# A third of layer 1's later weight pieces are split on GpSimd instead of VectorE

## The reference

```
h    = modulate(rmsnorm(x)); proj = h @ w_in        # 1024 x 3856, in three groups of columns
y    = concat(ssd(proj), attention(proj), hyena(proj))
x    = x + g1 * (y @ w_out)
x    = x + g2 * swiglu(modulate(rmsnorm(x)))        # w_gu, w_down
```

## Time and profile before

| | |
|---|---|
| median of 3 runs | 1210.33 us (1209.53 to 1211.54) |
| the profiled execution's own time | 1211.26 us |
| span of that execution | 1209.2 us |
| PE busy | 1175.9 us, 97% |
| DVE busy | 826.8 us, 68% |
| ACT busy | 527.9 us, 44% |
| POOL busy | 16.3 us, 1% |
| `w_lo` on DVE (L1861) | 220 operations, 264.2 us |

### The profile page before, as it was taken

One profiled execution on the slowest core, in us unless ns is written; L12 is line 12 of the kernel. 1 busy time (PEld: TensorE's weight loads), 2 busy tenths in 40 slices (PEclk: granted clock), 3 DMA queues, 4 the chain that ended last, 5 costly groups with the idle time before them and its releaser, 6 DMA issues. The chain is left out here.

```text
span 1209.2 us, 16485 instructions
## 1 busy us (share of the span) xinstructions
PE 1175.9 (97%) x6628; PEld 952.8 (79%) x6628; DVE 826.8 (68%) x1297; ACT 527.9 (44%) x911; POOL 16.3 (1%) x35
## 2 busy tenths in 40 slices
PE   6999999999999999999999999999989999999998
PEld 4768777787667778888887778779888788889887
DVE  5746467869766838777656666575699876776674
ACT  4534544642544532231122323264785555443454
POOL 0000000000100000000000000000000010000000
PEclk9999999999999999999999999999999999999999
DMA  9843244421012255565565454323434224655653
GB/s 337 271 136 128 89 138 132 147 70 53 18 36 70 70 173 168 184 206 191 174 220 186 163 180 160 112 71 94 136 105 123 71 71 139 191 183 184 191 175 123
DMA packets 132419, 171.35 MB, mean 142 GB/s; under 512 B 9300, under 2 KB 112374, under 8 KB 132344
## 3 DMA queue, kind: packets, MB, share of 16 engines
q1 hardware_dynamic: 131860, 170.12, 43.9%
q10 hardware_dynamic: 484, 0.18, 0.1%
HBM read 169.24 MB, written 1.05 MB: 141 GB/s over the span
## 5 line engine op out<-in xcount | busy, mean ns | idle before, releaser
L1861 DVE TENSOR_TENSOR w_lo<-w_raw,w_hi 128x1024 fp32r<-128x1024 f32 (+2 forms) x220 | 264.2, 1206 | 148.6 <-ACT w_hi L1480 146.5
L1480 ACT ACTIVATE w_hi<-w_raw 128x1024 fp32r<-128x1024 f32 (+2 forms) x220 | 228.5, 1042 | 292.5 <-DMA w_raw<-in_w_gu_dram 140.6
L736 PE MATMUL ps<-h_hi,w_hi 128*128 128x512 f32 (+1 forms) x576 | 218.4, 379 | 1.5 <-ACT gate L1788 0.8
L738 PE MATMUL ps<-h_hi,w_lo 128*128 128x512 f32 (+1 forms) x576 | 212.7, 369 | 0.0
L737 PE MATMUL ps<-h_lo,w_hi 128*128 128x512 f32 (+1 forms) x576 | 212.4, 369 | 0.0
L736 PE MATMUL ps<-f_hi,w_hi 128*128 128x512 f32 (+1 forms) x472 | 167.7, 355 | 2.1 <-DVE xT L2290 1.6
L738 PE MATMUL ps<-f_hi,w_lo 128*128 128x512 f32 (+1 forms) x472 | 162.5, 344 | 0.0
L736 PEld LDWEIGHTS ps<-h_hi,w_hi 128*128 128x128 f32 x576 | 108.5, 188 | 28.3 <-issue 9.6
L738 PEld LDWEIGHTS ps<-h_hi,w_lo 128*128 128x128 f32 x576 | 108.4, 188 | 18.8
L737 PEld LDWEIGHTS ps<-h_lo,w_hi 128*128 128x128 f32 x576 | 108.6, 189 | 17.4
L747 PE MATMUL ps<-h_hi,w_hi 128*128 128x512 f32 x320 | 113.3, 399 | 0.6 <-DVE w_lo L1861 0.6
(11 more groups left out here) (346 smaller groups left out, 1871.6 us busy)
## 6 DMA issues: line engine op xcount, KB each, us to landing
w_raw<-in_w_gu_dram SPq DMA_DIRECT2D x88, 512.0 KB, 3.6
w_raw<-in_w_in_dram SPq DMA_DIRECT2D x60, 512.0 KB, 3.7
w_raw<-in_w_down_dram SPq DMA_DIRECT2D x32, 512.0 KB, 3.5
m_even<-in_w_mod_dram SPq DMA_DIRECT2D x14, 1024.0 KB, 5.8
m_odd<-in_w_mod_dram SPq DMA_DIRECT2D x14, 1024.0 KB, 5.8
m_raw<-in_w_mod_dram SPq DMA_DIRECT2D x24, 512.0 KB, 5.5
m_first<-in_w_mod_dram SPq DMA_DIRECT2D x16, 512.0 KB, 10.4
w_raw<-in_w_out_dram SPq DMA_DIRECT2D x16, 512.0 KB, 3.4
```

What stands on the lines that cost most here:

```text
L736: mm(o, w_hi[:, i % RING, w], hi[:, 0:n], start=first and k == 0, stop=False)
L738: last = mm(o, w_lo[:, i % RING, w], hi[:, 0:n], start=False, stop=final and k == nk - 1)
L1480: A(w_hi[:, i % RING, w], w_raw[:, i % RING, w], ACT.Copy).then_inc(w_hi_done, 1)
L1861: TT(w_lo[:, i % RING, w], w_raw[:, i % RING, w], w_hi[:, i % RING, w].bitcast(F32), ALU.subtract).then_inc(w_lo_done, 1)
```

## The change

Five pieces, 125, 128, 131, 134 and 137 (the ones that DVE splits in slots 13, 16, 19, 22 and 25 of layer 1), are now split by GpSimd, with the same subtraction on the same tiles. GpSimd waits for `w_hi_done` and signals a new semaphore `w_lo_pool`. DVE skips them. Since `w_lo_done` now counts only DVE's pieces, PE's waits go through `lo_ready(count)`, which waits for the right number of each; from piece 126 on, every such wait of PE is two.

```diff
+POOL_SPLITS = [PLAN[1, "in"][0] + s + 2 for s in (13, 16, 19, 22, 25)]
...
+        w_lo_pool = sem("w_lo_pool")
...
         @block.gpsimd
...
+                for i in POOL_SPLITS if l == 1 else ():
+                    pool.wait_ge(w_hi_done, i + 1)
+                    w = slice(0, piece_cols(i))
+                    nc.gpsimd.tensor_tensor(w_lo[:, i % RING, w], w_raw[:, i % RING, w], w_hi[:, i % RING, w].bitcast(F32),
+                                            ALU.subtract).then_inc(w_lo_pool, 1)
                 p.after("hy_sq", 2)
...
+            def lo_ready(count):
+                by_pool = sum(i < count for i in POOL_SPLITS)
+                pe.wait_ge(w_lo_done, count - by_pool)
+                if by_pool > 0:
+                    pe.wait_ge(w_lo_pool, by_pool)
...
-                            pe.wait_ge(w_lo_done, i + half + 1)
+                            lo_ready(i + half + 1)
...
             def split_w(i):
-                if i < PIECES:
+                if i < PIECES and i not in POOL_SPLITS:
```

More of the change, by code:

```diff
@@ L799, in first_half @@
                     part(k, w_hi, h_hi, k == 0)
-                pe.wait_ge(w_lo_done, g + 2)
+                lo_ready(g + 2)
                 for k in range(2):
@@ L828, in h_pair @@
                 for half in range(int(first), 2):
-                    pe.wait_ge(w_lo_done, g + 2 * half + 2)
+                    lo_ready(g + 2 * half + 2)
                     def of_hi(k, c):
@@ L1139, in _ @@
                             if u == 0:
-                                pe.wait_ge(w_lo_done, i + 2)
+                                lo_ready(i + 2)
                                 pair_open(q)
@@ L1166, in part_half @@
                     if j == 0:
-                        pe.wait_ge(w_lo_done, g0 + i + 1)
+                        lo_ready(g0 + i + 1)
                     if i > 0:
@@ L1318, in _ @@
                     i = g0 + PARTS + ch
-                    pe.wait_ge(w_lo_done, i + 1)
+                    lo_ready(i + 1)
                     if ch >= 2:
```

## The result

The changed kernel took 1216.55 us (median of 6 runs, 1215.77 to 1218.21), the kernel before 1211.21 us beside it (6 runs, 1209.53 to 1212.29). The ratio is 1.0045, interval 1.0035 to 1.0056: 5.3 us slower (4.2 to 6.8). The forecast was 1213.5 with a range of 1209.2 to 1215.6: the sign is right, and the time lies 0.95 us above the range. Of the 3.05 us between forecast and result, 0.88 is the base (the kernel before had a median of 1210.33 in the runs shown and 1211.21 in these) and 2.1 is the effect itself, 5.3 instead of 3.2.

A forecast was written before the change was run, and what follows sets the result against it. PE bounds most of the kernel, DVE is nearer at 880.4 to 922; 0.76 + 0.40 + 2.18 + 2.15 - 2.28 = +3.2 us on 1211.26 gives 1214.5, median 0.93 lower: 1213.5 us, range 1209.2 to 1215.6.

The forecast's parts named there:

- Duration on GpSimd: One 1024-wide split on POOL: 2.35 us, on a line through the 256-wide and 512-wide additions.
- the dear bound of 2.94: Upper bound for one POOL split, four 256-wide additions: 2.94 us; as a rival +5.5 us, 1215.9, chance 0.08.
- Exclusion: POOL and DVE operations with two SBUF inputs exclude each other for a whole instruction; no-exclusion rival 1208.0 us, chance 0.11.
- Holds of 125, 128, 131, 134: Delays from DVE held by POOL: `em` twice, +0.76 and +0.40; split of 130, 2.18; rotations and `hbuf`, 2.15 us.
- The choice that POOL gets in behind the DVE operation in flight: For pieces 131 and 134, POOL gets in at the first end of a DVE operation: +3.2 us in all, chance 0.50.
- the rival: DVE keeps the port while its operations follow each other: holds 0.53 and 0.36, in all -0.2 us, 1210.1; chance 0.27.
- the order of asking: At the port POOL and DVE are served as they came; POOL comes 0.4 us before the split of 130.
- Relief: DVE time freed per split, 1.14 us: 131 and 134 count in full, 2.28 us; 125, 128 and 137 count 0.
- the argument that PE would then wait for the rounding of piece 141: Behind the 0.33 us wait at 921.19, PE would wait for ACT's rounding instead, so 137's relief counts 0.
- The waits: PE's 93 extra waits on `w_lo_pool`, 15 in this stage and 78 behind: 0 us; rival 1.9 us, 1215.4, chance 0.04.
- Piece 137: Rounded at 910.66, POOL to 913.1 beside DVE operations with one PSUM operand; split at 913.01 hardly touched: 0.
- a late ACT: Named as a way to be wrong: a late DVE makes ACT late too; no size given.

The follow-up runs named there:

- the kernel of its own: Separate kernel with nothing of the program: GpSimd subtractions alone, then beside four kinds of VectorE chains; 1024 columns took 2.34 us alone.
- the kernel with the relief alone: Changed kernel without the GpSimd splits: nobody makes the five rests, PE multiplies `w_hi` instead; 1207.66 us, ratio 0.9977 to the kernel before.
- the filled pause: Changed kernel with 20 matmuls, output unread, in front of the `em` product of slot 20; 1215.07 us, ratio 1.0040 to the kernel before.
- the one in which GpSimd held `hyv`: Changed kernel with only pieces 132 and 134 on GpSimd, 134 only behind DVE's `hbuf`; 1209.82 us, ratio 0.9985 to the kernel before.

## Why the prediction was right in sign and too low in size

- **Duration on GpSimd.** Predicted 2.35, measured 2.34 alone and 2.38 to 2.40 in place. The line through the two shorter sizes was the right choice, and the dear bound of 2.94 was not needed.
- **Exclusion.** Right. `em`, the split and `hbuf` were held, and DVE operations with a PSUM input were not. The rule of the Trainium skill ("SBUF — State Buffer", Who interferes with whom) holds in this case, in the program and in the kernel of its own (3.36 us against 1.22; 0.68 where one input lies in PSUM).
- **Holds of 125, 128, 131, 134.** Predicted 0.76, 0.40, 2.18, 2.15; measured 0.80, 0.53, 2.30 and 2.07. The choice that POOL gets in behind the DVE operation in flight was right for 131. For 134 it was right only in the result: the four short rotations did keep POOL out, as the rival has it, but only 0.4 us of them were left, and then `hbuf` was open. In the kernel of its own a chain of 28 kept it out for 5.2 us, so the order of asking, from which the prediction argued, does not decide by itself. That this price came out right is partly luck: it hung on POOL asking near the end of the chain.
- **Relief.** The 2 x 1.14 for 131 and 134 came as 2.25 in the kernel with the relief alone, and as 1.11 and 1.15 in the whole. 137's was set to 0 and is worth 0.48 to 0.58: the argument that PE would then wait for the rounding of piece 141 was wrong in this size.
- **The waits.** Counted as 0, and 0 within 0.1% was measured.
- **The step that failed.** Piece 137: "the next split, at 913.01, is hardly touched: 0". It was worked out from the times of before, in which POOL ends at 913.1 and the split of 136 starts at 913.01. The prediction itself had made ACT, PE and DVE late by different amounts: in after POOL starts 6.5 us later than that (917.32 against 910.78), and the split of 136 only 5.4 later (918.40 against 913.01). POOL's interval then lies across the split and holds it for 1.2, which costs PE 0.93. With the relief of 0.48 that is a net +0.45 where 0 was forecast. The prediction had named a late ACT as not priced; this is where it told. The rows show why ACT was later than DVE. Piece 137 goes into the buffer of piece 133, which PE releases at the end of slot 23, just ahead of its second wait for `hbuf`. That end was at 905.95 in before and is at 912.44 in after, 6.5 us later. ACT then waits for the load, 1.08 instead of 0.51 us:

```profile
916.18 1.06 ACT L1496 ACTIVATE w_hi<-w_raw 128x1024 fp32r<-128x1024 f32 x1 [1.08 <-DMA w_raw<-in_w_in_dram]
```

  DVE, which no longer had piece 134 to split, had made up 1.1 us of the delay by then; the load of 137 had not.
- **The term that is missing.** The sum has nothing for PE's own clock behind a pause of PE. In both profiles of the changed kernel the 2.5 us pause was followed by 3.4 us at half speed, worth 1.58 us of the 5.47. The remaining 0.23 us are small differences in the other terms (+0.17 for the two `em`, +0.12 and -0.08 in the holds of 131 and 134, +0.02 in the reliefs).

With 3.21 + 0.45 + 1.58 + 0.23 the account reaches the 5.47 of the profile. What stays open is the clock's share in the median. The half clock came in the first profile of after, in the second, and twice as long in that without 137; it did not come in the kernel with only piece 131, whose pause is as long. Over all their runs the changed kernel (both groups) and the one without 137 have a mean granted clock of 0.9962 to 0.9968, the kernel before 0.9974 to 0.9979. If PE lost all of it, the difference of about 0.001 would be some 1.2 us, near the 1.58. But single runs of one kernel lie between 0.994 and 0.999, and among the 110 runs of these kernels a clock lower by 0.001 goes with a span only 0.5 us longer than that of the same kernel's other runs, so by that estimate the clock's share in the medians is nearer 0.5 us. The profiles show where the other part comes from: half-clock stretches of 3.4 or 6.8 us between 23 and 31 us in five of them (131 alone among them) and of 3.4 us from 58.8 us on in that of the changed kernel run again, and in none of those of before, of after and of the filled pause. In these six the profile starts 0.7 to 2.9 us late, in the others at most 0.6. How the 2.1 us by which the effect was missed divide between piece 137 and the clock in the medians stays open; in the profiles it is 0.45 and 1.58.

## What to carry to other kernels

Before an idle GpSimd is given two-input work, look at what DVE does in that window: long two-input operations and ones that wait were held here for all of GpSimd's 2.3 us, operations with a PSUM input weren't, and what is freed on DVE is worth only the waits of TensorE behind it (2.8 us for all five pieces here, against 6.6 us of holds). Place such work from the shifted timeline and not from the old one: once some parts are late, the order of arrival of the next ones changes, as it did for piece 137. And price a new pause of TensorE twice, once for its length and once for the clock that may be half behind it.

## What the hardware showed that I had not expected

- A chain of short DVE operations without waits keeps GpSimd from the port for as long as it lasts: 28 of 128 columns made a 2.34 us operation take 7.58. Long ones (1024 columns) alternate with it, 3.2 to 3.4 us each.
- TensorE's granted clock fell to half (1.2 GHz) 0.4 to 1.6 us behind pauses of 2.49 us (two profiles) and 2.16 us (one), while the engine was busy again, for 3.4 us each time; in a fourth profile it fell in the last 0.3 us of a pause of 2.50 us and stayed low for 6.8 us. Behind pauses of 2.49 and 2.32 us in two other kernels it stayed at 2.4 GHz. The Trainium skill ("TensorE: Matmul & The Clock Gate", Part 1) says that the gate judges recent activity by a window of time that runs free of the kernel's start. That would make the same pause cheap in one execution and dear in another; no run here tests it.
- A wait answers only to what is freed inside its own stretch: PE's wait for `st` was 1.48 to 1.50 us in every kernel but the one in which GpSimd held `hyv`. In the profile of before, DVE works without a pause for 3.8 us between the end of `hbuf` and the end of `st` (short convolutions and `st`, no split among them), and PE has 2.2 us of work from the start of the one product to the start of the other. A split that is freed ahead of `hbuf` moves both products and leaves the wait between them.
